# State-space decays from two wide matmuls of split running sums, in a two-layer hybrid trunk

## What is computed

```python
acum = jnp.cumsum(dtk * a, axis=1)
seg = acum[:, :, None] - acum[:, None, :]
decay = jnp.exp(jnp.where(causal[None, :, :, None, None], seg, -jnp.inf))
cb = jnp.einsum('btgn,bsgn->btsg', cf, bf)
xdt = xf * dtk[..., None]
y_diag = jnp.einsum('btsgr,bsgrp->btgrp', cb[..., None] * decay, xdt)
```

## Time and profile before

| | |
|---|---|
| runs | 1601.16, 1601.34, 1609.09 us; median 1601.34 |
| the profiled execution | 1601.24 us, of which the profile's span is 1599.5 |
| mean granted clock | 0.977 of full |
| PE, DVE, ACT busy in the span | 96%, 77%, 64% |
| the state-space loop, from its first projection to the last chunk of the output projection before PE waits for the residual | 395.9 to 605.4 us of the span |

### The profile page before, as it was taken

One profiled execution on the slowest core, in us unless ns is written; L12 is line 12 of the kernel. 1 busy time (PEld: TensorE's weight loads), 2 busy tenths in 40 slices (PEclk: granted clock), 3 DMA queues, 4 the chain that ended last, 5 costly groups with the idle time before them and its releaser, 6 DMA issues.

```text
span 1599.5 us, 21555 instructions
## 1 busy us (share of the span) xinstructions
PE 1541.1 (96%) x7791; PEld 1301.6 (81%) x7791; DVE 1235.1 (77%) x1069; ACT 1023.6 (64%) x943; POOL 60.9 (4%) x97
## 2 busy tenths in 40 slices
PE   7899999999999897999999999999999999999997
PEld 6788888888999875788888888888888888888885
DVE  6555555455798755898898898898898898898996
ACT  5455444346577543777877877777777776777774
POOL 2015000000000000100000000000000000000020
PEclk9799999999999898999999999999999999999999
DMA  9149855545443232999999999999999999999997
GB/s 340 57 140 396 327 179 184 203 157 161 132 133 106 106 123 76 375 383 380 386 380 377 384 383 368 394 378 377 385 386 376 385 375 383 378 380 385 414 387 293
DMA packets 166233, 476.25 MB, mean 298 GB/s; under 512 B 9153, under 2 KB 35025, under 8 KB 166177
## 3 DMA queue, kind: packets, MB, share of 16 engines
q1 hardware_dynamic: 157152, 446.73, 75.3%
q0 software_dynamic: 5888, 19.23, 3.1%
q10 hardware_dynamic: 3136, 9.54, 1.5%
HBM read 454.49 MB, written 20.97 MB: 297 GB/s over the span
## 4 chain that ended last, share of the span: by engine, by line
PE 85%; DVE 6%; DMA 3%; ACT 2%; issue 2%; DVEq 1%; SPq 0%; ACTq 0%
PE bank L745 26%; PE bank L747 26%; PE bank L746 26%; DMA ring<-moe_w_gu_in 2%; DVE w_lo L1290 2%; DVE acc L1581 1%; PE bank L1173 1%; DMA ring<-swa_w_qkv_in 1%; ACT w_hi L434 1%; DVE arg L1605 1%; PE bank L855 1%; DVE w_lo L1651 1%; PE bank L1091 1%; PE bank L764 0%; PE bank L1160 0%
## 5 line engine op out<-in xcount | busy, mean ns | idle before, releaser
L1651 DVE TENSOR_TENSOR w_lo<-ring,w_hi 128x2048 fp32r<-128x2048 f32 x336 | 763.5, 2289 | 84.8 <-PE bank L747 74.1
L641 ACT ACTIVATE w_hi<-ring 128x2048 fp32r<-128x2048 f32 x336 | 636.3, 1920 | 150.4 <-DMA ring<-moe_w_gu_in 95.1
L745 PE MATMUL bank<-w_hi,xgT_hi 128*128 128x512 f32 x896 | 351.6, 392 | 3.4 <-DVE w_lo L1651 2.3
L747 PE MATMUL bank<-w_hi,xgT_lo 128*128 128x512 f32 x896 | 349.7, 390 | 0.0
L746 PE MATMUL bank<-w_lo,xgT_hi 128*128 128x512 f32 x896 | 349.3, 390 | 0.0
L1290 DVE TENSOR_TENSOR w_lo<-ring,w_hi 128x2048 fp32r<-128x2048 f32 (+1 forms) x84 | 190.0, 2265 | 121.2 <-ACT w_hi L434 120.6
L434 ACT ACTIVATE w_hi<-ring 128x2048 fp32r<-128x2048 f32 (+1 forms) x84 | 159.0, 1898 | 122.2 <-PE bank L747 115.4
L745 PEld LDWEIGHTS bank<-w_hi,xgT_hi 128*128 128x128 f32 x896 | 168.7, 188 | 38.3 <-DVE w_lo L1651 2.7
L747 PEld LDWEIGHTS bank<-w_hi,xgT_lo 128*128 128x128 f32 x896 | 168.6, 188 | 35.4
L746 PEld LDWEIGHTS bank<-w_lo,xgT_hi 128*128 128x128 f32 x896 | 168.6, 188 | 34.3
L745 PE MATMUL bank<-w_hi,m_hT_hi 128*128 128x512 f32 x448 | 175.8, 392 | 0.0
(11 more groups left out here) (299 smaller groups left out, 1710.2 us busy)
## 6 DMA issues: line engine op xcount, KB each, us to landing
ring<-moe_w_gu_in SPq DMA_DIRECT2D x230, 1024.0 KB, 7.1
ring<-moe_w_down_in SPq DMA_DIRECT2D x112, 1024.0 KB, 7.3
ring<-ffn_w_gu_in SPq DMA_DIRECT2D x28, 1024.0 KB, 6.8
ring<-ffn_w_down_in SPq DMA_DIRECT2D x14, 1024.0 KB, 4.8
xg_rows<-zeros POOLq DMA_DIRECT2D x36, 256.0 KB, 12.3
ring<-ssm_w_in_in SPq DMA_DIRECT2D x8, 1024.0 KB, 5.0
ring<-ssm_w_in_in SPq DMA_DIRECT2D x16, 512.0 KB, 3.8
ring<-ssm_w_in_in SPq DMA_DIRECT2D x32, 256.0 KB, 4.3
```

Of the source, the lines that this page charges most:

```text
L641: act.activation(w_hi[:, c % HI], ring[:, c % RING], ACT.Copy).then_inc(hi_ready, 1)
L745: pe.matmul(o, stat[0], mov[0], start=start, stop=False)
L747: return pe.matmul(o, stat[1], mov[0], start=False, stop=stop)
L1651: dve.tensor_tensor(w_lo[:, c % SPLIT], ring[:, c % RING], w_hi[:, c % HI].bitcast(F32), ALU.subtract).then_inc(lo_ready, 1)
```

## The change

For each head the decay's exponent is computed by PE instead of DVE. At set-up the running sums of all heads are transposed (three 128 x 128 transposes) and each is split in a rounded part and the rest; rows of the two parts stand one below the other in the same tile (`decay_parts`). A row mask for the group gives a stationary tile `decay_stat` (three blocks of 128), made for each group by an ACT copy with a scale (`of_group`); `decay_mov` holds the sums with their signs, once for all. One matmul of 512 columns, `decay_stat` by `decay_mov`, then gives the differences of the sums for four heads of a block; ahead of it, for the diagonal blocks, a matmul of `after` (-2^100 where the key is later than the query) by four identities masks them. So a group has 2 + 2 matmuls of 512 columns for the diagonal blocks and one for the cross block, all in fp32r, in place of 8 of 128 columns in fp32.

The exponentials read the banks: two for the diagonal blocks, and a third for the cross block, whose matmul (`cross_decay`) stands between the two halves of the projection of step g+2, in the bank of the first diagonal block. DVE's `arg` and `CBm` go; `M` is three instructions that read C B from bank 5 as it is, four heads to one block. `yT_hi` and `yT_lo` move ahead of the step's last weight split, and the cross block's exponential and product stand behind that split. The small sums of dt*a move ahead of the last part of z on PE. The masks (six reductions of the identity) are made on DVE at the start of the dense block. `decay_parts` stands on DVE between the splits of chunks GR0+1 and GR0+2; `decay_of` lies in the tile `zeros`, so it waits for POOL's clearing transfers.

```diff
@@ PE, ahead of the loop
+                if n == 3:
+                    pe.wait_ge(c_dtA, 1)
+                    (the three small sums, inc c_acol)
                 times_1024(Z0 + 2 * n, ...)
-            pe.wait_ge(c_dtA, 1)
-            (the three small sums, inc c_acol)
             pe.wait_ge(c_zs, 6)
+            pe.wait_ge(c_sums, 1)
+            for b in range(3):
+                ins = pe.transpose(bank[6][:, b * P:(b + 1) * P], M[:, 0, b], ident[:])
+            ins.then_inc(c_sumsT, 1)
@@ PE, the loop
+            def cross_decay(g):
+                pe.wait_ge(c_exp0, 2 * g + 1)
+                pe.matmul(bank[4][:], decay_stat[:, g % 2, 2], decay_mov[:, 1], start=True, stop=True).then_inc(c_abx, 1)
                     for half in range(2):
+                        if half == 1 and s >= 2:
+                            cross_decay(s - 2)
                         have(GR0 + 2 * s + half)
...
                     for c in range(3):
                         out_product(c, (0,))
+                        if c == 0:
+                            cross_decay(G - 2)
...
+                    pe.wait_ge(c_stat, g + 1)
                     for t in range(TT):
-                        for r in range(REP):
-                            ins = pe.matmul(bank[4 + t][:, r * P:(r + 1) * P],
-                                            dtA[:, t, g * REP + r:g * REP + r + 1].to_broadcast([P, P]), tri[:],
-                                            start=True, stop=True)
+                        pe.matmul(bank[4 - t][:], after, ident_r.unsqueeze(1).to_broadcast([P, REP, P]),
+                                  start=True, stop=False)
+                        ins = pe.matmul(bank[4 - t][:], decay_stat[:, g % 2, t], decay_mov[:, t], start=False, stop=True)
                     ins.then_inc(c_abc, 1)
...
                 if s == G:
-                    pe.wait_ge(c_xd, 2 * G)
+                    pe.wait_ge(c_xd, G)
+                    pe.wait_ge(c_exp0, 2 * G)
                     for c in range(3):
                         out_product(c, (1,))
+                        if c == 0:
+                            cross_decay(G - 1)
@@ ACT, the loop, behind the silu of step s
                 g = s - 1
                 if 0 <= g < G:
-                    act.wait_ge(c_arg, g + 1)
-                    act.activation(arg[:, 0:2], arg[:, 0:2], ACT.Exp)
-                    for r in range(REP): (one Exp of 128 columns each, inc c_exp)
-                if s < G:
-                    ahead(GR0 + 2 * s + 4)
+                    if g == 0:
+                        act.wait_ge(c_parts, 1)
+                        act.activation(decay_stat[:, 0], decay_of, ACT.Copy, scale=of_group[:, 0:1]).then_inc(c_stat, 1)
+                    if g >= 1:
+                        act.wait_ge(c_m, g)
+                    act.wait_ge(c_abc, g + 1)
+                    (Exp of bank 4 to arg[:, 0], then of bank 3 to arg[:, 1], each inc c_exp0)
+                    if g + 1 < G:
+                        (decay_stat of g + 1, inc c_stat)
                 (squares and yT_hi of s - 3)
+                if s < G:
+                    ahead(GR0 + 2 * s + 4)
+                g = s - 1
+                if 0 <= g < G:
+                    act.wait_ge(c_abx, g + 1)
+                    (Exp of bank 4 to arg[:, 2], inc c_exp)
@@ DVE, the loop
-                    (arg: 8 instructions)
                     (Xdt and the skip term, as before)
-                    (CBm: 3 instructions)
-                    dve.wait_ge(c_exp, g + 1)
-                    dve.tensor_tensor(M[:], arg[:], CBm[:].unsqueeze(2).to_broadcast([P, 3, REP, P]), ALU.mult)
-                if s < G:
-                    ahead(GR0 + 2 * s + 4)
+                    for b, of in ((0, 0), (1, 2)):
+                        dve.wait_ge(c_exp0, 2 * g + b + 1)
+                        dve.tensor_tensor(M[:, b], arg[:, b], cb[:, of].unsqueeze(1).to_broadcast([P, REP, P]), ALU.mult)
                 (yT_lo of s - 3)
+                if s < G:
+                    ahead(GR0 + 2 * s + 4)
+                (behind c_exp: M[:, 2] from arg[:, 2] and bank 5, inc c_m)
```

More of the change, by code:

```diff
@@ L31 @@
 AXX = mybir.AxisListType.X
+AXXY = mybir.AxisListType.XY
 P = 128
@@ L128, in build @@
                                     hT_lo=((KD, T), F32R))
+        _, decay_mov, decay_stat, after, ident_r = phase(
+            w_hi_again=((SPLIT, SLOT), F32R), decay_mov=((TT, REP, P), F32R), decay_stat=((2, 3, P), F32R),
+            after=((P,), F32R), ident_r=((P,), F32R))
         w_hi = sb("w_hi", [P, HI, SLOT], F32R)
@@ L610, in _ @@
                 if 0 <= g < G:
-                    act.wait_ge(c_arg, g + 1)
-                    act.activation(arg[:, 0:2], arg[:, 0:2], ACT.Exp)
-                    for r in range(REP):
-                        ins = act.activation(arg[:, 2, r], bank[5][:, r * P:(r + 1) * P], ACT.Exp,
-                                             bias=acol[:, 2 * SH + g * REP + r:2 * SH + g * REP + r + 1])
-                    ins.then_inc(c_exp, 1)
-                if s < G:
-                    ahead(GR0 + 2 * s + 4)
+                    if g == 0:
[4 more added lines that the diff above has]
+                    act.wait_ge(c_abc, g + 1)
+                    act.activation(arg[:, 0], bank[4][:].rearrange("p (r t) -> p r t", r=REP), ACT.Exp
+                                   ).then_inc(c_exp0, 1)
+                    act.activation(arg[:, 1], bank[3][:].rearrange("p (r t) -> p r t", r=REP), ACT.Exp
+                                   ).then_inc(c_exp0, 1)
+                    if g + 1 < G:
+                        act.activation(decay_stat[:, (g + 1) % 2], decay_of, ACT.Copy,
+                                       scale=of_group[:, g + 1:g + 2]).then_inc(c_stat, 1)
                 g = s - 3
@@ L627, in _ @@
                                        scale=vT[:, 32 + 2 * g + k:33 + 2 * g + k]).then_inc(c_yThi, 1)
+                if s < G:
[3 more added lines that the diff above has]
+                    act.wait_ge(c_abx, g + 1)
+                    act.activation(arg[:, 2], bank[4][:].rearrange("p (r t) -> p r t", r=REP), ACT.Exp).then_inc(c_exp, 1)
             ahead(MOE0 - 1)
@@ L1096, in _ @@
                     if g >= 1:
[L1097 removed]
+                        pe.wait_ge(c_xd, g)
                     for t in range(TT):
@@ L1561, in _ @@
             ahead(GR0)
+            dve.wait_ge(c_acol, 1)
+            dve.tensor_copy(acol[:, 0:2 * SH], bank[7][:, 0:2 * SH])
+            dve.drain()
+            dve.tensor_tensor(acol[:, 2 * SH:3 * SH], acol[:, 0:SH], bank[7][:, 2 * SH:3 * SH], ALU.subtract)
+            dve.drain()
+            sums = acol[:, 0:3 * SH].rearrange("p (b h) -> p b h", b=3).unsqueeze(2).to_broadcast([P, 3, 4, SH])
+            dve.tensor_copy(M[:, 0, 0:3].rearrange("p b (q h) -> p b q h", q=4), sums).then_inc(c_sums, 1)
             for half in range(2):
@@ L1566, in _, with decay_parts @@
             ahead(GR0 + 1)
-            dve.wait_ge(c_acol, 1)
-            dve.tensor_copy(acol[:, 0:2 * SH], bank[7][:, 0:2 * SH])
-            dve.drain()
-            dve.tensor_tensor(acol[:, 2 * SH:3 * SH], bank[7][:, 2 * SH:3 * SH], acol[:, 0:SH], ALU.subtract)
-            dve.drain()
+            def decay_parts():
+                dve.drain()
+                dve.wait_ge(c_sumsT, 1)
+                whole = bank[6][:, 0:3 * P].rearrange("p (b s) -> p b s", b=3)
+                left = M[:, 1, 0:3]
+                dve.tensor_copy(decay_stat[:, 1], whole)
+                dve.drain()
+                rounded = decay_stat[:, 1].bitcast(F32)
+                dve.tensor_tensor(left, whole, rounded, ALU.subtract)
+                dve.drain()
+                dve.tensor_scalar(left, left, lower, None, ALU.mult)
+                dve.drain()
+                dve.scalar_tensor_tensor(left, rounded, upper, left, ALU.mult, ALU.add)
+                dve.drain()
+                dve.tensor_copy(ident_r, ident[:])
+                dve.tensor_scalar(after, tri_lt[:], -float(2 ** 100), None, ALU.mult)
+                dve.wait_ge(rows_cleared, 2 * (3 * E + 3) * 16)
+                dve.tensor_scalar(decay_of, left, bot, top, ALU.mult, ALU.add)
+                dve.tensor_scalar(M[:, 2, 0:TT], left[:, 0:TT], top, not_bot, ALU.mult, ALU.add)
+                dve.drain()
+                dve.tensor_tensor(decay_mov, M[:, 2, 0:TT].unsqueeze(2).to_broadcast([P, TT, REP, P]),
+                                  of_head.unsqueeze(1).unsqueeze(3).to_broadcast([P, TT, REP, P]),
+                                  ALU.mult).then_inc(c_parts, 1)
+            decay_parts()
+            ahead(GR0 + 2)
             dve.wait_ge(c_zs, 8)
-            ahead(GR0 + 2)
             for s in range(G + 3):
@@ L1598, in _ @@
                     hs = slice(g * REP, (g + 1) * REP)
-                    dve.wait_ge(c_abc, g + 1)
-                    if g >= 1:
-                        dve.wait_ge(c_m, g)
-                    for t in range(TT):
```

(5 more changed lines are left out.)

50 lines of the change are left out of this document (31 added, 19 removed).

## The result

The changed kernel takes 1587.53 us (median of four runs, 1584.88 to 1588.32), the kernel before 1603.37 timed beside it (four runs, 1601.16 to 1609.09): a ratio of 0.9896, 95% interval 0.9868 to 0.9924. By the ratio it is faster by 16.7 us (12 to 21), by the medians 15.8; 8.0 were forecast. The profiled execution took 1587.10 us, its span is 1585.4 against 1599.5, and the mean granted clock 0.985 against 0.977.

The account below looks back on a forecast made before the run. Loop paced by DVE through `yT_lo`, PE and DVE nearly even. Step 8's first chunk behind the last wait moves from 568.85 to 560.8, 8.1 us early, so 1601.24 becomes 1593.3 us; 8-in-10 range 1587.5 to 1600.5.

Parts of the forecast that it names:

- DVE was the pace by `yT_lo`, PE is it afterwards: State-space loop: PE's 9.3 us of waits for `yT_lo` go; a step becomes 16.82 us of PE plus 0.4 of wait.
- Wide fp32r matmuls at 0.23: Decay matmuls on PE: 0.23 us per 512 columns, so 0.92 + 0.23 a group in place of 1.84.
- The rival with the fp32 rate: Decay matmuls run at the fp32 rate, 0.69 us more on each of 40: 1621 us; chance 0.07.
- The wait of 9.1 us for `decay_stat`: PE waits from 422.2 to 431.3 us behind ACT's silu of step 1, plus 3.7 us of slow clock.
- ACT's two dates: Loop: first exponential ready at 10.5 us, PE there at 10.79; cross block's M at 17.7 against 17.2, wait 0.4.
- how near the rival was: ACT's chain becomes the loop's pace: with 1 us more on it 1600 us, beyond 1.1 slower than before; chance 0.08.
- Step 8's wait: PE waits 2.7 us at the cross matmul for the exponential, plus 3.5 for the clock.
- The last wait: Step 8: PE waits for both exponentials of group 7 behind a table load, 1.9 at most, 1.7 us taken.
- the rival of a third slow stretch: The clock falls behind step 8's final wait of 1.7 us, 3.3 more: 1596.6 us; chance 0.22.
- Set-up costs nothing: `decay_parts` (4 to 6 us on DVE) and the masks fit idle time: nothing taken, at most 1 us.
- Behind the stage, no change: After step 8's waits: one more cross matmul, 0.2 us, and the rest as it was.
- everything at the short end: No waits in the five steps (-2.0), step 8's wait at full clock (-3.5): 1587.8 us; chance 0.13.

Follow-up runs that it names:

- e7: Changed kernel with the cross block's matmul behind the projection instead of between its halves: 1604.05 us, ratio 0.9991 to the kernel before.
- e9: The changed kernel unaltered, run once more to see what repeats in a trace: 1587.13 us.
- e1: Changed kernel with the first group's `decay_stat` made by ACT at the end of step 0, not behind the silu of step 1: 1582.47 us.
- e3: Changed kernel with squares, `yT_hi` and `yT_lo` put back behind the cross block's exponential and product: 1589.61 us.
- e4: Changed kernel with PE made to wait in steps 4 and 6 ahead of the y transposes: 1603.49 us.
- e5: Changed kernel with PE made to wait in steps 4 and 6 behind C B, ahead of the projection: 1598.08 us.
- e6: Changed kernel with PE made to wait in steps 5 and 7 between the projection's halves: 1592.72 us.
- e8: e1 with group 0's cross matmul three us later and step 8's behind the second output chunk: 1579.82 us, the fastest.
- e2: Kernel before with only the squares, `yT_hi` and `yT_lo` moved ahead of the step's last weight split: 1596.39 us.
- e10: e8 with y's split put back as in e3, timed together with e11: 1581.01 us.
- e11: e8 run again unaltered, timed together with e10: 1580.54 us.

## Why the prediction was right, and where it failed

1. **DVE was the pace by `yT_lo`, PE is it afterwards**: right. No wait for `yT_lo` is left, five steps take 85.4 us where 86.1 was forecast, and in two of them PE is busy for 34.03 of 34.22 us and DVE for 29.59, 86% (85 was forecast). The 0.7 us between 86.1 and 85.4 are two misses that offset each other: waits of 0.4 us in place of 2.0, and 17.0 us of work in a step in place of 16.82. Of the latter 0.1 is that the first wide matmul of a group takes 0.32 us; the rest isn't taken apart.
2. **Wide fp32r matmuls at 0.23**: right; in step 7 they start at 536.76 (behind fp32 ones), 537.08, 537.31 and 537.54, and the loop's work fell by 5.3 of the 5.5 us. The rival with the fp32 rate is out. C B read from PSUM cost nothing either: in the groups of DVE's instructions (times, then busy us and mean ns) `M` with a bank takes less than `y` x `z` from SBUF. This is what the Trainium skill ("VectorE: DVE Perf Modes", The perf-mode tier table) gives, the same mode for a two-tensor fp32 operation from either memory, and not what its advice to copy first (Rules for kernel authors) would suggest.

```profile
L1690 DVE TENSOR_TENSOR M<-arg,bank 128x512 f32<-128x512 f32 x16 | 10.2, 679 | 0.0
...
L1670 DVE TENSOR_TENSOR y<-y,z 128x512 f32<-128x512 f32 x8 | 5.5, 692 | 0.7
```

3. **The wait of 9.1 us for `decay_stat`**: right, 8.95. Its clock was taken at 3.7; from the wait's end (432.35) to projection 2 (436.18) it took 3.83 in place of 1.93, and the first half of the projection 6.57 in place of 5.80: 2.7 in all, by the windows 2.8. The reason: the clock had fallen inside the wait, and what of the slow stretch PE spends idle costs nothing. The rows I took the price from were waits of 1.9 to 4.6 us.
4. **ACT's two dates**: right in the five steps, the wait for M being 0.2 twice instead of 0.4 each time. e7 shows how near the rival was: with one matmul 5.8 us later PE waits for M in every step. The table load has no drain behind it here: it starts at 457.23, lasts 1.28, and the exponential starts at 458.53. The Trainium skill ("ScalarE: Activation LUTs", What ACT_TABLE_LOAD costs) adds a drain of some 1380 ns at each switch, and the trace doesn't agree. With it in the chain, an estimate from the page's figure and the prediction's 17.7 against 17.2 us, every step would have waited for M by over a microsecond; three didn't wait and two waited 0.2.

```profile
457.23 1.28 ACT L628 ACT_TABLE_LOAD   x1
458.53 0.60 ACT L628 ACTIVATE arg<-bank 128x512 f32<-128x512 f32 x1
```

5. **Step 8's wait**: 2.7 forecast, 2.37 measured; but **the 3.5 us of clock behind it is the step that failed**. The clock stayed. "Since 1.89 us was enough for it" took one row for a rule, though the earlier trace rows held a wait of 3.08 us without a slow stretch. The same wait (2.37 to 2.39) had none in three traces (changed, e9, e1), and one in e3, e4, e5 and e6, with 1.5 to 1.7 us lost: neither 3.5 nor sure. So the wait was right, and what the runs showed in place of the 3.5 is 0 here and at most 1.7 elsewhere; what decides between them stays open.
6. **The last wait**: 1.7 forecast, 0.86 measured, and for another reason. I had PE wait for both exponentials of group 7, with a table load of 1.28 ahead of them. That load isn't there: in step 8 no silu stands between group 6's exponentials and group 7's, so the set is in place. The exponentials end at 555.36, and PE starts at 556.13. What ends its wait is DVE, which `c_xd` stands for in the same place: its last skip term of y ends at 556.07. The prediction left this date out. The clock behind it stayed at 1.00, so the rival of a third slow stretch is out. The rows of ACT, then of DVE:

```profile
554.28 0.60 ACT L628 ACTIVATE arg<-bank 128x512 f32<-128x512 f32 x1 [7.17 <-PE bank L1129]
554.77 0.59 ACT L630 ACTIVATE arg<-bank 128x512 f32<-128x512 f32 x1
...
555.66 0.41 DVE L1682 TENSOR_TENSOR y<-bank,dsk 128x256 f32<-128x256 f32 x1
```

7. **Set-up costs nothing**: right. The last of `decay_parts` ends at 406.4, the split behind it follows at once, and DVE still idles 1.26 us ahead of the taps. The loop starts 0.86 later than before, but the same program up to there gave 1.05 in e9 and -1.16 in e1, so it can't be laid to the change.

```profile
405.25 1.23 DVE L1644 TENSOR_TENSOR decay_mov<-M,sm 128x1024 fp32r<-128x1024 f32 x1
406.40 2.28 DVE L1329 TENSOR_TENSOR w_lo<-ring,w_hi 128x2048 fp32r<-128x2048 f32 x1
409.94 1.28 DVE L1656 SCALAR_TENSOR_TENSOR acc<-U,cwT,acc 128x256 f32<-128x256 f32 x3 [1.26 <-ACT U L609]
```

8. **Behind the stage, no change**: nearly. 42.53 for 42.28 is the cross matmul's 0.2; the part with `h` is 1.1 shorter by shorter slow stretches (4 us in place of 8), the experts 0.6. The 1.1 isn't shown to be the change's: the two stretches last 4 to 5 us in the traces of the changed kernel, e9 and e1, and 7 to 8 in all others, e3 and the faster e8 among them.

In the loop the sum gave 8.1 us and 13.6 were measured. Of the 5.5 between, 0.8 arise up to projection 3 (the clock, item 3, less 0.2), 0.7 in the five steps, and 4.0 in step 8: 3.5 of clock, 0.3 and 0.85 of its two waits, less 0.6 of work that the sum had too short. So four fifths are the clock's. The rival "everything at the short end" (1587.8) was this case, at 0.13; it should have had as much as the forecast, since the rows of before held punished and unpunished waits alike. That its number fits so closely is in part luck: it took 2.0 us off the five steps, where 0.7 came, and left the price of the first slow stretch and the last wait as they were, where another 1.85 came.

The larger miss is one of reading. I counted a gain of 9.3 us of waits and found it eaten by a new 9.1, and looked on the clock as an addition to each wait. The sum of the waits stayed, and most of the gain, 8.4 of 13.6 us, was that fewer of them brought the clock down and that part of the one slow stretch fell into a wait.

## What to carry to other kernels

Count PE's waits one by one with the clock behind each: four waits of 2 to 5 us (12.4, and 11.2 of clock) cost twice as much as one of 9 (and 2.8), and those below 1.3 us mostly cost only themselves. Where a new small tile is needed by PE, look at what stands ahead of its making in the other engine's row (a silu of 1.7 us and its wait, here 9 us), and make it a step early. When a price is taken from one row, look for a row that contradicts it and let both set the chances.

## What the chip showed that I had not expected

The same wait can be followed by half clock or not, and by very different amounts of it. PE's waits in the loops of these traces, with the busy time lost to the clock behind each:

| wait, us | what stands behind it | lost to the clock |
|---|---|---|
| 0.46, 1.03, 1.03, 1.24 (e2) | y transposes | 0 |
| 0.85 to 1.06 (the last wait, and e8's, e10's and e11's others) | output chunks, projection, y transposes | 0 |
| 0.92 (e8) | M x Xdt | 1.7 |
| 0.92 (e10, e11), 0.97 (e7, five times) | M x Xdt | 0 |
| 1.41 (e7) | M x Xdt | 3.4 |
| 1.53 (e10) | y transposes | 0 |
| 1.20 (e6, twice), 1.4 to 1.5 (all, twice; once more in e2) | projection; in e2 output chunks | 0 |
| 1.89, 2.77 (before) | y transposes | 3.4 each |
| 2.37 (changed, e9, e1) | cross matmul, output chunks | 0 |
| 2.37 to 2.39 (e3, e4, e5, e6), 2.83 (e7) | the same | 1.4 to 1.7 |
| 2.51 (e1) | cross matmul, projection | 1.6 |
| 2.76 (e5, twice) | projection | 1.7 each |
| 2.90 (e2) | output chunks | 1.4 |
| 3.08 (before) | output chunks | 0 |
| 3.22 (e4, twice) | y transposes | 5.1, 4.8 |
| 4.62, 4.66 (before, e2) | y transposes | 4.4, 4.9 |
| 8.95 (changed, e3 to e7, e9) | wide matmuls, transposes | 2.5 to 3.0 |

The length of a wait doesn't settle it, nor does the work behind it: 1.41 us was followed by 7 us of slow clock and 1.53 by none. What else does, the moment at which the wait falls for one, is left open; two executions of one kernel agreed inside the loop and differed in its first 20 us. With nothing changed in a kernel its time differs by up to 6.6 us from run to run, and its mean clock with it (e10: 1578.03 at 0.986, 1584.66 at 0.981), more than the smaller edits here do.
